# A modulation product moved from the matrix engine to VectorE, in column chunks

## What is computed

```
mod = jnp.einsum('bd,de->be', jax.nn.silu(c), w_ada[l]) + b_ada[l]      # c: (1, 1024), w_ada: (1024, 6144)
sh1, sc1, g1, sh2, sc2, g2 = [m[:, None, :] for m in jnp.split(mod, 6, axis=-1)]
h = _rms(x, norm1_g[l]) * (1.0 + sc1) + sh1
```

## Time and profile before

| | |
|---|---|
| device time, median of 3 runs | 1911.99 us (1909.17 to 1913.01) |
| span of the profiled execution, first to last instruction | 1910.2 us |
| PE / PEld busy | 1819.2 us (95%) / 1032.4 us (54%) |
| DVE / ACT / POOL busy | 601.7 us (31%) / 477.1 us (25%) / 351.5 us (18%) |
| DMA | 582.89 MB, mean 305 GB/s |
| chain that ended last | PE 75%, DMA 14%, DVE 7%, ACT 3% |

### The profile page before, as it was taken

One profiled execution on the slowest core, in us unless ns is written; L12 is line 12 of the kernel. 1 busy time (PEld: TensorE's weight loads), 2 busy tenths in 40 slices (PEclk: granted clock), 3 DMA queues, 4 the chain that ended last, 5 costly groups with the idle time before them and its releaser, 6 DMA issues.

```text
span 1910.2 us, 27104 instructions
## 1 busy us (share of the span) xinstructions
PE 1819.2 (95%) x11233; PEld 1032.4 (54%) x11233; DVE 601.7 (31%) x1224; ACT 477.1 (25%) x800; POOL 351.5 (18%) x306
## 2 busy tenths in 40 slices
PE   8999999999998899999999999999999898899998
PEld 8987999777976333323332233322322697644443
DVE  6777555337566300100010000000000787501112
ACT  5854443325322110000000010000000565322121
POOL 3000000000000599999940000000000100100000
PEclk9998999998999999999999999999999899999999
DMA  6555657446733999999999999999999451579996
GB/s 196 156 142 185 198 197 239 153 134 212 263 111 132 394 419 415 420 419 420 412 418 420 420 418 408 419 420 420 415 418 402 111 168 62 220 308 420 420 419 281
DMA packets 152740, 582.89 MB, mean 305 GB/s; under 512 B 11673, under 2 KB 77866, under 8 KB 109600
## 3 DMA queue, kind: packets, MB, share of 16 engines
q1 hardware_dynamic: 150000, 575.09, 77.3%
q0 software_dynamic: 2608, 5.97, 1.2%
HBM read 579.96 MB, written 1.05 MB: 304 GB/s over the span
## 4 chain that ended last, share of the span: by engine, by line
PE 75%; DMA 14%; DVE 7%; ACT 3%; issue 2%; SPq 0%; ACTq 0%; DVEq 0%
PE ps L1814 18%; PE ps L437 9%; PE ps L438 9%; PE ps L439 9%; DMA ring<-in_moe_w_out 8%; PE ps L2312 6%; PE ps L1807 5%; PE ps L1846 4%; PE ps L2336 3%; DMA ring<-in_moe_w_in 3%; PE ps L2275 2%; PE ps L1726 1%; DVE wlo L480 1%; PE ps L1850 1%; DMA more<-in_moe_w_in 1%
## 5 line engine op out<-in xcount | busy, mean ns | idle before, releaser
L1814 PE MATMUL ps<-ring,xg 128*64 128x512 f32 x1638 | 405.8, 597 | 5.4 <-DMA ring<-in_moe_w_in 2.7
L480 DVE TENSOR_TENSOR wlo<-raw,whi 128x2048 fp32r<-128x2048 f32 (+5 forms) x95 | 209.5, 2208 | 175.9 <-ACT whi L462 175.6
L1814 PEld LDWEIGHTS ps<-ring,xg 128*64 128x64 f32 x1638 | 121.2, 136 | 248.0 <-issue 240.6
L462 ACT ACTIVATE whi<-raw 128x2048 fp32r<-128x2048 f32 (+4 forms) x96 | 177.0, 1847 | 176.9 <-PE ps L439 82.2
L437 PE MATMUL ps<-xh,whi 128*128 128x272 f32 (+1 forms) x712 | 210.4, 296 | 0.9 <-DVE wlo L857 0.9
L1846 PE MATMUL ps<-ring,ahm 128*64 128x512 f32 x808 | 203.5, 597 | 6.9 <-DMA ring<-in_moe_w_out 6.8
L439 PE MATMUL ps<-xh,wlo 128*128 128x272 f32 (+1 forms) x712 | 208.6, 293 | 0.0
L438 PE MATMUL ps<-xl,whi 128*128 128x272 f32 (+1 forms) x712 | 208.3, 293 | 0.0
L2237 POOL TENSOR_SCALAR lnt<-lnt,h 128x384 f32<-128x384 f32 x120 | 188.6, 1572 | 12.2
L1987 DVE TENSOR_TENSOR sgm<-sgm,ps 128x512 f32<-128x512 f32 x28 | 17.5, 683 | 496.7 <-PE ps L1814 496.7
L437 PEld LDWEIGHTS ps<-xh,whi 128*128 128x128 f32 (+1 forms) x712 | 133.4, 187 | 4.1 <-issue 2.4
(11 more groups left out here) (584 smaller groups left out, 2368.3 us busy)
## 6 DMA issues: line engine op xcount, KB each, us to landing
ring<-in_moe_w_in SPq DMA_DIRECT2D x117, 1024.0 KB, 19.9
ring<-in_moe_w_out SPq DMA_DIRECT2D x101, 1024.0 KB, 20.0
ring<-in_moe_w_in SPq DMA_DIRECT2D x117, 768.0 KB, 11.5
ring<-in_w_gate SPq DMA_DIRECT2D x29, 1024.0 KB, 13.1
raw<-in_ffn_w_in SPq DMA_DIRECT2D x28, 1024.0 KB
ring<-in_w_down SPq DMA_DIRECT2D x26, 1024.0 KB, 12.0
raw<-in_w_ada SPq DMA_DIRECT2D x24, 1024.0 KB
ring<-in_w_up SPq DMA_DIRECT2D x20, 1024.0 KB, 9.5
```

The source lines that it names most:

```text
L462: e.activation(whi[0:rows, s % NSPL, 0:n], raw[0:rows, i % NRAW, 0:n], ACT.Copy).then_inc(S.hi.s, S.hi.up((s,)))
L480: e.tensor_tensor(wlo[0:rows, s % NSPL, 0:n], raw[0:rows, i % NRAW, 0:n], whi[0:rows, s % NSPL, 0:n].bitcast(F32), ALU.subtract).then_inc( ...
L1814: ins = e.matmul(ps_[b][64 * v:64 * v + 64, :], a[:, j, 64 * v:64 * v + 64], both[v][:, 0, 512 * b:512 * b + 512], start=j == 0, stop=j == 7)
```

## The change

The 24 chunks of `w_ada` become 24 column chunks: all 1024 rows of 256 columns. DVE multiplies each 256-column slice of the eight in a chunk by its silu(c) scalar and adds it to one of two accumulators (even and odd slices), eight instructions in all (`dve_ada_sum`). PE then sums over the 128 partitions: four float32 matmuls whose stationary operand is a 128 by 128 piece of an accumulator and whose moving operand is one column of ones (`pe_ada_sum`); the result comes out as columns. ACT copies the bank once for four chunks (`act_ada`), and DVE adds the whole bias once (`dve_ada`). A `raw` slot with such a chunk is free when DVE has summed it. The places change too:

- chunks 0 to 12: one in each of the FFN iterations 1 to 13. In the stream chunk j stands behind the up chunk of iteration j + 1; DVE sums it at the end of its iteration j; PE adds it up in iteration j + 1 between gate and up
- 13 to 18: in the down projection, in the stream behind chunk 1, 3, ... 11 of it; DVE before its split in steps 0, 2, ... 10; PE behind steps 0, 2, ... 10
- 19 to 23: behind `gv` 2, `gv` 3, `gr` 0, 1 and 2
- none in RG, none from `gr` 3 on

```diff
-            part = w_ada[256 * (j % 4):256 * (j % 4) + 256, 1024 * (j // 4):1024 * (j // 4) + 1024]
-            M.add(("ada", j), 128, CW, by_rows(part, 0, 2, 1024), split=False)
+            M.add(("ada", j), 128, CW, by_rows(w_ada, 256 * j, 8, 256), split=False)
...
-    plan_ada(2)
     for j in range(6):
         M.add(("ro", j), 112, CW, by_blocks(w_ro, j, 112), keep=True)
...
-        plan_ada(2 if j == 0 else 1 if j in FFN_ADA else 0)
-    plan_ada(2)
+        plan_ada(1 if j else 0)
     for j in range(14):
         M.add(("ffn", "d", j), 128, CW, by_blocks(d["ffn_w_out"][0], j, 128), keep=True)
+        plan_ada(1 if j - 1 in DOWN_ADA else 0)
...
+                if S.chunks[i - NRAW][0][0] == "ada":
+                    e.wait_ge(dve.s, dve.at(*S.chunks[i - NRAW][0]))
+                elif p is None or i - NRAW in S.kept:
...
+    ada_acc = [[a[:, 0:256], a[:, 256:512]] for a in (row1, ada1)]
+    def dve_ada_sum(e, j):
+        i = M.index["ada", j]
+        w = raw[:, i % NRAW, :].rearrange("p (k n) -> p k n", k=8)
+        if j == 0:
+            e.wait_ge(act.s, act.at("silc"))
+        if j >= 2:
+            e.wait_ge(pe.s, pe.at("adac", j - 2))
+        e.wait_ge(M.raw[i % NRAW].s, M.raw[i % NRAW].at(i))
+        for k in range(8):
+            o = ada_acc[j % 2][k % 2]
+            if k < 2:
+                e.tensor_scalar(o, w[:, k, :], silc[:, k:k + 1], None, ALU.mult).then_inc(dve.s, dve.up())
+            else:
+                e.wait_ge(dve.s, dve.n - 1)
+                e.scalar_tensor_tensor(o, w[:, k, :], silc[:, k:k + 1], o, ALU.mult, ALU.add).then_inc(dve.s, dve.up(("ada", j)))
+    def pe_ada_sum(e, j):
+        g, r = j // 4, j % 4
+        p = bank("adac", g) if r else bank.take(e, "adac", g)
+        e.wait_ge(dve.s, dve.at("ada", j))
+        for i in range(2):
+            for a in range(2):
+                ins = e.matmul(p[:, 2 * r + i:2 * r + i + 1], ada_acc[j % 2][a][:, 128 * i:128 * i + 128],
+                               cst[:, C_SM + 1:C_SM + 2], start=a == 0, stop=a == 1)
+        ins.then_inc(pe.s, pe.up(("adac", j)))
...
# pe_ffn, gate and up
+                if j and nm == "g":
+                    pe_ada_sum(e, j - 1)
# pe_ffn, down, behind the 'used' of chunk j
+            if j in DOWN_ADA:
+                pe_ada_sum(e, 13 + DOWN_ADA.index(j))
# dve_ffn
             if j == 0:
                 dve_ln_finish(e, "ln0", 0, TILES)
                 dve.label(("ln0", "full"))
-            if j in (3, 13):
-                dve_ada(e, j // 13)
+            if j < 13:
+                dve_ada_sum(e, j)
         for j in range(13):
+            if j in DOWN_ADA:
+                dve_ada_sum(e, 13 + DOWN_ADA.index(j))
             split_lo(e, M, s)
```

More of the change, by code:

```diff
@@ L25 @@
 GROUPS = [(0, 2048), (2048, 1536)]
-FFN_ADA = (4, 6, 8, 10)
+DOWN_ADA = (0, 2, 4, 6, 8, 10)
+GLA_ADA = (("gv", 2), ("gv", 3), ("gr", 0), ("gr", 1), ("gr", 2))
 LAMBDA_INIT = 0.8 - 0.6 * math.exp(-0.3 * 0)
@@ L240, in build @@
             M.add((nm, j), 128, CW, by_rows(w_gl, o + 256 * j, 8, 256))
+            plan_ada(1 if (nm, j) in GLA_ADA else 0)
     for j in range(4):
         M.add(("go", j), 128, CW, by_blocks(d["gla_w_out"][0], j, 128))
-    plan_ada(8)
+    assert next(n_ada, None) is None
     def moe_order(ne, F):
@@ L339, in build @@
     early = ExitStack()
-    silp = early.enter_context(nc.sbuf_tensor("silp", [128, 8, 32], F32))
+    ada1 = early.enter_context(nc.sbuf_tensor("ada1", [128, 512], F32))
     vT = ph("vT", [112, 12, 8])
@@ L606, in pe_ada @@
         if r == 3:
-            bank.give(("ada", g), (act, "ada_row", g))
+            bank.give(("adac", g), (act, "ada_col", g))
     def act_ada(e, g):
[L610 to L628, removed]
+        e.wait_ge(pe.s, pe.at("adac", 4 * g + 3))
+        e.activation(modc[:, 8 * g:8 * g + 8], bank("adac", g)[:, 0:8], ACT.Copy).then_inc(act.s, act.up(("ada_col", g)))
@@ L630, in pe_meta_rows, with dve_ada @@
+    def dve_ada(e):
+        e.wait_ge(act.s, act.at("ada_col", 5))
+        e.tensor_tensor(modc[:, :], modc[:, :], colA[:, 64:112], ALU.add).then_inc(dve.s, dve.up(("mod",)))
     def pe_meta_rows(e, p, key, parts):
@@ L848, in act_setup @@
         e.wait_ge(dve.s, dve.at("col"))
-        e.activation(silp[:, :, 0:1], silc.unsqueeze(2), ACT.Silu).then_inc(act.s, act.up(("silc",)))
+        e.activation(silc, silc, ACT.Silu).then_inc(act.s, act.up(("silc",)))
     def dve_setup(e):
         e.memset(rowB, 0.0).then_inc(dve.s, dve.up(("rowB",)))
-        e.memset(silp[:, :, :], 0.0).then_inc(dve.s, dve.up())
         dve_turn(e, "x0", TILES, 5, xh, xl)
@@ L907, in pe_rg @@
         pe_rg_in(e, "gb", "gelu")
-        for j in range(2):
-            pe_ada(e, j)
         acc = {(t, q): bank.take(e, "ln0", t, q) for t, _, _ in XTILES for q in range(2)}
@@ L1188, in act_ffn @@
                 e.activation(g, bank("fg", f)[:, 0:T], ACT.Silu).then_inc(act.s, act.up(("fg", f)))
+                if f in (8, 16, 24):
+                    act_ada(e, f // 8 - 1)
                 e.wait_ge(dve.s, dve.at("fu", f))
                 e.activation(fah[:, f, :], g, ACT.Copy).then_inc(act.s, act.up(("fa", f)))
-            if j in (0, 10):
-                act_ada(e, j // 10)
         for j in range(13):
+            if j == 6:
+                act_ada(e, 3)
             split_hi(e, M, s)
@@ L1289, in pe_gla @@
         bank.give(("gz",), (act, "zT"))
-        for j in (10, 11):
-            pe_ada(e, j)
         p = bank.take(e, "bg")
@@ L1303, in pe_gla @@
         pe_chan(e, "gk", 1)
-        for j in (12, 13):
-            pe_ada(e, j)
-        pe_ada_columns(e, 2)
         pe_chan(e, "gq", 0)
         pe_chan(e, "gq", 1)
-        for j in (14, 15):
-            pe_ada(e, j)
         for j in range(2):
             pe_tokm(e, "gv", j, TILES, 256)
-        pe_ada_columns(e, 3)
         e.wait_ge(dve.s, dve.at("gk", 3))
@@ L1329, in pe_gla @@
             pe_tokm(e, "gv", j, TILES, 256)
+            pe_ada_sum(e, 17 + j)
         for j in range(3):
             pe_tokm(e, "gr", j, XTILES, 256)
+            pe_ada_sum(e, 21 + j)
         e.wait_ge(act.s, act.at("gv", 3, 1))
@@ L1355, in pe_gla @@
         pe_tokm(e, "gr", 3, XTILES, 256)
-        for j in (16, 17):
-            pe_ada(e, j)
         p = {}
@@ L1375, in pe_gla @@
         pe_rows_out(e, "go", acc, XTILES, "x3", 2)
-        pe_ada(e, 18)
         pe_last_two(e, "ln2", acc, None, [("go", 2), ("go", 3)],
                     lambda m, cc, n: (xh[:, 4 + m, cc:cc + n], xl[:, 4 + m, cc:cc + n]), [])
-        for j in range(19, 23):
-            pe_ada(e, j)
-        pe_ada_columns(e, 4)
         pe_turn_tiles(e, "x4", "ln2", QTILES, 8, 6, by_turns)
@@ L2183, in dve_route1_end @@
         dve.label(("gates", "of place"))
-        dve_ada(e, 5)
+        dve_ada(e)
         dve_over(e)
```

36 lines of the change are left out of this document (7 added, 29 removed).

## The result

The changed kernel takes 1945.05 us (median of 4 runs, 1938.51 to 1951.32), the kernel before in the same set 1910.58 us (4 runs). The ratio is 1.0173, 95% interval 1.015 to 1.0197: 34.5 us slower. The forecast was +17.4 us and a range up to 1942; the direction was right, the size half of what came.

What follows compares the result with a forecast made beforehand. It took PE, with a few DVE and ACT chains, to set the first expert load at 619.93 us. Terms: -13.0 - 6.7 + 22.1 + 5.5 + 7.5 + 2.0 = +17.4, giving 1929 us; own range 1922 to 1938, 8-in-10 range 1914 to 1942.

Steps and rivals of the forecast that it cites:

- What was removed: Old products on PE's path ahead of GLA and in its output projection: removing them gives 13.0 us back.
- The sum on PE: Four one-column matmuls per chunk, 0.92 us each sum; all 24 on the path, 22.1 us added.
- the rejection of 25 ns a matmul: The skill page's 25 ns a matmul would make a sum 0.2 us; the forecast priced the weight loads instead.
- The chunk on DVE: DVE's eight instructions take 2.9 us a chunk, covered in steady FFN iterations.
- PE's wait for chunk 0: In FFN iteration 1 PE waits once for DVE, which finishes the layer norm first: 5.5 us.
- The waits in the down projection: PE waits 1.4 us with each of sums 14 to 18 for load and DVE sum: 7.0 us.
- The last chunk of the projection: Down projection: its slot is freed late by the same rule, adding some 0.5 us.
- GLA's front: GLA's first part: `gv` starts earlier, a row-copy wait and a column step go, PE waits at `gq`; 6.7 us gained.
- The clock: Last layer norm: without the old products as filler, transposes and router run at half clock, losing 2.0 us.
- The sum now: Whole kernel: the forecast's terms, gains of 13.0 and 6.7 against costs, summed to +17.4 us.
- Behind the load: After the first expert load, some 17 us later than 619.93, the rest of the run stays as long.
- the rival in which DVE becomes the bound: Gate and up: DVE's sums come after PE asks, also costing more in the down part; +33 us, 1945; chance 0.12.

Runs made afterwards that it cites:

- the kernel with pauses: Kernel before with five idle PE waits of 1.19 us in the down projection, each followed by four one-column matmuls: 1925.18 us, ratio 1.0069.
- the filler: Changed kernel plus four matmuls of 512 columns on constants under PE's wait for the last layer norm: 1946.96 us.
- the version without stalls: Changed kernel with later, halved sums, none in FFN iterations 0 and 1, and a filler at the last norm: 1906.93 us, repeated 1909.07.

## Why the prediction was wrong, point by point

- **What was removed.** The start of the FFN moved forward by 1.5 us (157.52 for 159.05; forecast 2.05). Kernels with the same code up to there start it up to 3 us apart, but the means of the two groups, 156.8 and 158.3, differ by 1.5 as well. The output projection of GLA lost its 1.2 us: from the turn behind the gated norm to that behind the last norm it is 31.2 us instead of 32.54. Right.
- **The sum on PE**, 0.92 forecast, 0.9 measured three ways (iterations of 13.0 for 12.1; 0.45 less for half of it; 0.90 in the kernel with pauses). Right, and with it the rejection of 25 ns a matmul.
- **The chunk on DVE**, 2.9 us, and PE's wait for chunk 0, 5.5 us: right. The half clock behind that wait, 19 matmul starts from 190 to 194 where some 32 fit, cost 2.3 us and had no term (the next sum comes 15.3 us later instead of 13.0).
- **The waits in the down projection: the step that failed.** "PE waits 1.4 us, with sums 14 to 18, 7.0 us" prices only the time in which PE stands still. The mechanism and the place were right, the size was low: 10.75 us of waits, of which 2.3 are one slow load and the rest 0.3 us more for each wait. Behind each wait the clock fell to 0.50, which cost 10.4 us more and had no term at all. The two kernels that differ only in asking later and in filling the wait show that both parts hang on PE's standing still: without the waits both are gone, with the waits filled the clock stays up and 11.1 us come back.
- **The last chunk of the projection**, 0.5 forecast: PE did not wait for it in the changed kernel. The wait of 1.99 us is only in the version with later sums.
- **GLA's front.** PE waited for DVE's split at `gq` as forecast, and lost 1.5 to 2 us more to the clock behind it. `gv` starts 44.4 us behind the turn for 47.1 before, 2.8 earlier instead of 5.1; up to the gated norm GLA gave 0.4 us back, not the forecast's net 2.1 (6.7 less five sums).
- **The clock.** The forecast gave it one place, the last layer norm, 2.0 us; measured 2.4, and the filler brought 1.8 back. That place was found because an old filler was removed from it. The new waits that the forecast itself named were not looked at with the same eye, though the window at 575 showed what follows a wait.
- **The sum now.** 17.4, and on top of it the clock in the down projection 10.4, the waits there 3.7, the clock behind chunk 0 2.3, GLA's front 1.7, the last norm 0.4 and the start of the FFN 0.5; off it the last chunk 0.5, the 19 sums of the FFN at 0.89 instead of 0.92 0.6, the output projection 0.1, and 2.0 by which iteration 0 ended sooner behind the turn (20.5 us for 22.6) in these two executions. This last part is chance: the half clock at the start of the FFN lies from 156 to 167 here and from 162 to 173 in the kernel before, and in the other kernels the stretch took 20.9 to 22.6 us. Together 33.2 us; at the first expert load 33.5 are measured.
- **Behind the load** the forecast had no change. The profiled execution took 1295.75 us there against 1290.3. In the other kernels, with the same code from there on, it was 1285.9 to 1292.4. In the changed kernel 4.7 us of it lie between 1607 and 1673, at a mean clock of 0.87 against 0.94. Why it fell there is not settled, nor was it tried.

The time of 1945 is that of the rival in which DVE becomes the bound. That the number agrees is chance, since its mechanism isn't what happened: a chunk took DVE 2.9 us, not 3.8 or 4.6, and no sum from the third iteration to the end of gate and up was waited for.

The rule of the Trainium skill that the forecast cited ("TensorE: Matmul & The Clock Gate", section "HAM oscillation") describes a loop that idles for a load in each round and is slowed behind each idle time anew. That is the down projection here, and these traces agree in kind: some 3.5 us at 0.50 from 378.7 on, behind the wait at 377.46, and again four times. They do not agree that it happens each time: behind the pauses of 1.95 and 2.71 us it was five times of ten. The forecast used it for a filler that was taken away and not for the loop that it was written for.

## What to carry to other kernels

When a forecast puts a new wait on PE, it should carry a second term for the clock behind it, here 1.3 to 1.6 us a fall in the kernels with pauses and 2.1 us a wait in the changed one, taken from a place in the old trace where PE had to wait in like work; and it should say that the term comes by chance, which widens the range. A reduction by one-column matmuls is not free on PE: 0.11 us a record here, so let DVE add its accumulators first. When the wait cannot go, ask for the result a step later before thinking of a filler, and size a filler by the wait that is left after all other edits.

## What the runs showed of the hardware that was not expected

- Equal pauses in equal work do not have equal consequences: three falls of the clock in five pauses of 1.95 us, two in five of 2.71 us, none in five of 1.19 us, three in five of 1.19 us with four one-column matmuls behind, in the one profiled execution of each. The changed kernel's four runs lie 12.8 us apart and those with later sums 1.4, but the waits do not explain the spread alone: with the waits filled and the clock at 1.00 in the profile it is 11.6 us.
- A fall lasts some 3.5 us in most cases. It was 7 us behind two of the waits of the changed kernel, though PE worked on without a gap once those waits had ended.
- A wait of 1.99 us at the end of the down projection of the version with later sums left the clock at 1.00, and one of 2.61 us at the same place in the version without stalls was followed by 0.50 from 429 to 433. In the second set of that version, the same code, the wait was 2.12 us and the clock stayed at 1.00.
